# Fetching each expert row as two indirect DMAs, one per table, instead of one

## The reference

```
# scores of 8 heads against two sets of 128 keys; the best 16 of each; the best 16 of the 256 sums
idx = cand_i[best 16]                 # 16 expert numbers for each token and head, out of 16384
g   = softmax(top_s)
u   = take(u_tab, idx)                # 16384 x 1024 float32
a   = gelu(dot(u, h))                 # one number for each token and expert
vv  = take(v_tab, idx)                # 16384 x 1024 float32
out = sum over 128 experts of (g * a) * vv
```

## Time and profile before

| | |
|---|---|
| median of 3 runs | 2637.37 us (2637.25 to 2637.92) |
| the profiled execution, its own time | 2638.77 us |
| its span, first to last instruction | 2637.0 us |
| first expert row issued to last one landed, first layer | 1204.36 to 1854.20 us |
| the same in the second layer | 1962.49 to 2614.21 us |
| PE, DVE, ACT, POOL busy | 88%, 58%, 28%, 22% |

### The profile page before, as it was taken

One profiled execution on the slowest core, in us unless ns is written; L12 is line 12 of the kernel. 1 busy time (PEld: TensorE's weight loads), 2 busy tenths in 40 slices (PEclk: granted clock), 3 DMA queues, 4 the chain that ended last, 5 costly groups with the idle time before them and its releaser, 6 DMA issues.

```text
span 2637.0 us, 24279 instructions
## 1 busy us (share of the span) xinstructions
PE 2324.4 (88%) x8188; PEld 1496.0 (57%) x8188; DVE 1528.5 (58%) x3683; ACT 742.6 (28%) x2126; POOL 581.6 (22%) x526
## 2 busy tenths in 40 slices
PE   8999999999989999998998777877889988778776
PEld 6688888876878888566443323322674433233222
DVE  3743642255446413446777778776448777677774
ACT  2232100122120013333333333432324333233332
POOL 0000000000000000003453443543014443534431
PEclk9999999999999999999999999999999999999999
DMA  7315586442438754217999999999649999999996
GB/s 294 131 36 216 193 307 269 175 148 85 159 124 315 300 198 160 96 64 322 420 419 417 420 412 421 403 421 421 252 176 420 420 420 420 415 419 414 409 421 259
DMA packets 92317, 777.45 MB, mean 295 GB/s; under 512 B 10272, under 2 KB 11424, under 8 KB 11936
## 3 DMA queue, kind: packets, MB, share of 16 engines
q0 software_dynamic: 73728, 536.90, 49.3%
q1 hardware_dynamic: 18464, 238.99, 23.7%
HBM read 774.80 MB, written 1.05 MB: 294 GB/s over the span
## 4 chain that ended last, share of the span: by engine, by line
DMA 28%; PE 19%; POOL 5%; DVE 5%; issue 3%; ACT 2%; POOLq 0%; ACTq 0%
DMA weight_ring<-tables,arena 16%; DMA arena<-tables,arena 11%; PE misc L1371 7%; PE tile L295 3%; PE tile L1297 3%; POOL arena L1527 3%; POOL weight_ring L1527 2%; PE tile L308 2%; DVE weight_ring L1501 1%; DVE arena L1501 1%; PE tile L1648 1%; PE tile L1647 1%; PE misc L1671 1%; PE tile L318 1%; ACT arena L1453 0%
## 5 line engine op out<-in xcount | busy, mean ns | idle before, releaser
L1371 PE MATMUL misc<-arena 128*128 128x512 f32 x1216 | 586.1, 619 | 141.6 <-ACT arena L1453 141.5
L1527 POOL DMA_INDIRECT arena<-tables,arena x304 | 322.9, 1062 | 1031.4 <-DVE arena L1149 882.4
L1371 PE MATMUL misc<-weight_ring,arena 128*128 128x512 f32 x832 | 393.6, 611 | 106.5 <-ACT arena L1453 106.2
L1501 DVE CUSTOM_DVE_ANT_0 arena<-arena,memT 128x1024 f32<-128x1024 f32 x304 | 371.2, 1225 | 189.2 <-DMA arena<-tables,arena 186.1
L1371 PEld LDWEIGHTS misc<-arena 128*128 128x128 f32 x1216 | 226.3, 195 | 434.8 <-ACT arena L1453 227.2
L295 PE MATMUL tile<-xT,weight_ring 128*128 128x256 f32 x1792 | 388.6, 379 | 0.0
L295 PEld LDWEIGHTS tile<-xT,weight_ring 128*128 128x128 f32 x1792 | 340.3, 190 | 47.9 <-issue 1.8
L1527 POOL DMA_INDIRECT weight_ring<-tables,arena x208 | 255.8, 1230 | 429.4 <-DVE arena L1149 366.0
L1501 DVE CUSTOM_DVE_ANT_0 weight_ring<-weight_ring,memT 128x1024 f32<-128x1024 f32 x208 | 254.2, 1224 | 149.3 <-DMA weight_ring<-tables,arena 148.7
L1371 PEld LDWEIGHTS misc<-weight_ring,arena 128*128 128x128 f32 x832 | 150.6, 192 | 321.8 <-ACT arena L1453 181.1
L1439 ACT ACTIVATE arena<-arena 128x2 f32<-128x2 f32 x256 | 52.1, 204 | 813.0 <-DVE arena L1501 812.9
(11 more groups left out here) (261 smaller groups left out, 2279.7 us busy)
## 6 DMA issues: line engine op xcount, KB each, us to landing
weight_ring<-panels SPq DMA_DIRECT2D x110, 2048.0 KB, 7.8
arena<-tables,arena POOLq DMA_INDIRECT x304, 15.0
weight_ring<-tables,arena POOLq DMA_INDIRECT x208, 18.9
arena<-c_rows SPq DMA_DIRECT2D x2, 1024.0 KB, 21.3
cst<-consts SPq DMA_DIRECT2D x1, 1224.0 KB, 26.6
xT<-acts SPq DMA_DIRECT2D x1, 1024.0 KB, 5.0
memT<-acts SPq DMA_DIRECT2D x1, 1024.0 KB, 11.5
arena<-acts SPq DMA_DIRECT2D x1, 1024.0 KB, 13.3
```

The lines of the kernel that those rows point to most:

```text
L1371: ins = nc.tensor.matmul(M[2 * a + b][:, :], diag[:, s % NDIAG, :], slot(rows, s)[:, D + b * 512:D + (b + 1) * 512], start=first_row, stop ...
L1501: nc.vector.tensor_tensor_reduce(out=u, in0=u, in1=ht[:, n // PH, :], scale=1.0, scalar=0.0, op0=ALU.mult, op1=ALU.add, accum_out=dot[:, c ...
L1527: pool.indirect_dma_start(slot(rows, s), None, tables, bass.IndirectOffsetOnAxis(idx[:, n % 2, k:k + 1], 0)).then_inc(landing(rows, s), 16)
```

## The change

The joined table is taken apart into `table_u` and `table_v`. Each row is fetched by two indirect DMAs of 4 KB to a partition, u first and then v, with the same expert numbers and into the same places as before. Each slot has two semaphores now, one for u and one for v. DVE waits for u alone, and PE has a wait for v ahead of its matmuls. The order of the rows, the slots and all other work stay as they are. The further lines reuse 22 semaphores of the first block, which has ended by then, since each slot needs one more.

```diff
+        spare = []
+
         def sem(name):
             if name not in sems:
-                sems[name] = ctx.enter_context(nc.semaphore(name))
+                sems[name] = spare.pop() if spare else ctx.enter_context(nc.semaphore(name))
             return sems[name]
...
+        for name in ("low_filled", "low_read", "z_filled", "z_made", "act_gate", "bc_made", "bd_made", "ep_made", "en_made",
+                     "ed_made", "kd_made", "qe_made", "kdt_filled", "kdt_read", "att_filled", "att_masked", "tap_added",
+                     "conv_made", "state_half", "osq_made", "gated", "o_scaled"):
+            spare.append(sems.pop(name))
...
-        def landing(rows, s):
+        def landing(rows, s, part):
             kind, i = rows.place[s]
-            return sem(f"row_landed{i if kind == 'near' else HOME + i}")
+            return sem(f"row_landed_{part}{i if kind == 'near' else HOME + i}")
...
                 pe.wait_ge(sem("diag_made"), HEADS * TOPK * l + s + 1)
+                pe.wait_ge(landing(rows, s, "v"), 16 * rows.landed[s])
...
-                    dve.wait_ge(landing(rows, s), 16 * rows.landed[s])
+                    dve.wait_ge(landing(rows, s, "u"), 16 * rows.landed[s])
...
-                pool.indirect_dma_start(slot(rows, s), None, tables,
-                                        bass.IndirectOffsetOnAxis(idx[:, n % 2, k:k + 1], 0)
-                                        ).then_inc(landing(rows, s), 16)
+                at = bass.IndirectOffsetOnAxis(idx[:, n % 2, k:k + 1], 0)
+                pool.indirect_dma_start(slot(rows, s)[:, 0:D], None, table_u, at
+                                        ).then_inc(landing(rows, s, "u"), 16)
+                pool.indirect_dma_start(slot(rows, s)[:, D:2 * D], None, table_v, at
+                                        ).then_inc(landing(rows, s, "v"), 16)
...
-            "tables": np.concatenate([a["peer_u_2"], a["peer_v_2"]], axis=2).reshape(DEPTH * NEXP, 2 * D),
+            "table_u": a["peer_u_2"].reshape(DEPTH * NEXP, D), "table_v": a["peer_v_2"].reshape(DEPTH * NEXP, D),
```

More of the change, by code:

```diff
@@ L205, in at, with build_program @@
         return n % NBANK, n // NBANK
-def build_program(nc, panels, vec_a, vec_b, consts, mask_in, acts, tables, c_rows, out):
+def build_program(nc, panels, vec_a, vec_b, consts, mask_in, acts, table_u, table_v, c_rows, out):
     with ExitStack() as ctx:
```

## The result

The kernel after takes 2807.23 us (median of 4 executions, 2804.28 to 2814.37) against 2637.64 for the kernel before in the same measurement: 1.0635 times as long, with a 95% interval of 1.0621 to 1.0648. That is 170 us more. The forecast was 2812 and slower. The ratios, here and in the table of the experiments, leave out executions more than 1.5% above the fastest of their kernel, which matters for the halves by partition alone: their ratio is that of the two fastest of four executions, 3450.97 and 3490.50 us.

A forecast was written before the change was run, and what follows sets the result against it. The DMA engines were taken to bound the kernel before, POOL's issues the one after. +177.5 us for the slower rows less 2.9 for the early u made +174.6, on the median 2637.37 us 2812; range 2650 to 2920.

The forecast's parts named there:

- The bound: Expert steps: POOL needs 2.87 us a row against the DMA engines' 2.54 and becomes the bound; chance 0.66.
- The price of an issue: POOL's issue of half the bytes costs the full price, 1.130 us plus a 0.305 us gap, twice a row.
- The hold: POOL's issue starting inside a DVE dot product waits for its end: mean 1.13 us against median 0.94.
- The sum by layer: First issue to last landing of each layer grows to 739.5 us: 89.7 + 87.8 = 177.5 us extra.
- the terms of the forecast: End of a layer: issue 0.94 us, then 5.1 to landing, then 6.07 to the closing copy less about 1.4.
- The thin cover: Next head's expert numbers arrive about POOL's 15th row of 16; one row late would cost 86 us over 30 heads.
- The early u: End of each layer: DVE waits for u alone, which lands 1.43 us ahead of v; -2.9 us in all.
- The packets: DMA engines: 4 KB packets cost a row the same as 8 KB ones, at most 20 us more in 512 rows.
- the case in which the stream stays the bound: Expert steps: issue with gap below 1.27 us, so the DMA engines still set the pace; 2635 to 2655 us, chance 0.15.
- The share of DMA: Expert steps after the change: DMA engines' busy share falls to 2.54/2.87, 0.88, at 365 GB/s.

The follow-up runs named there:

- the halves by partition: Kernel before with each row fetched by two indirect DMAs of 64 partitions each, all 8 KB wide: 3502.92 us, 1.314 times the kernel before.
- the last pair: Kernel before with only the last two rows of each layer split, in the order u254, u255, v254, v255: 2637.5 us, ratio 0.9988.
- the one-input kernel: Kernel after with the dot product replaced by a plain sum of u, one SBUF input instead of two: 2670.18 us, ratio 1.0113.

## Why the prediction was right

**The bound.** That POOL becomes the bound was right, and is shown from both sides: fewer bytes change nothing, more issues cost in proportion, and issues that are not held give four fifths of the time back. All of the loss lies in the expert steps: the rest of the span is 1323.3 us before and 1323.0 after.

**The price of an issue.** Forecast 1.130 + 0.305 us, taken from the mean of before; measured 1.120 + 0.304. The u issues, of half the bytes, have the median of before, 0.937 us. For two issues that is 2.85 us a row instead of 2.87. That an issue of half the bytes costs the same was an argument in the prediction, since no row showed one; the runs bear it out.

**The hold.** That the mean hold carried over from before, 0.19 us beyond the median, to 0.18 is in part luck. The prediction backed it by scaling the 0.25 us of a head with the share of time that DVE is in a dot product, 42/49, and this scaling fails with four issues a row: there the share is 1.225/5.75, or 21%, which would give 0.11 us, and 1.133 - 0.947 = 0.19 was measured. The rule for a single issue holds with one exception. Of the issues of the kernel after, 308 begin 0.1 to 1.0 us after the start of such an instruction of 128 x 1024, and all are held. Of the 20 that begin in its first 0.1 us, the ten within 0.041 us of its start are not held, and the ten from 0.045 us on are; they take up to 1.99 us.

**The sum by layer.** From the first issue to the closing copy, before: 655.9 and 657.8 us (the second closing copy of before is at 2620.28). The prediction's terms give 739.5 + 4.6 = 744.1 for each. The closing copies after:

```profile
1939.37 0.69 DVE L1211 COPY memT<-misc 128x512 f32<-128x512 f32 x1 [4.83 <-PE misc L1379]
...
2784.98 0.69 DVE L1211 COPY memT<-misc 128x512 f32<-128x512 f32 x1 [4.83 <-PE misc L1379]
```

With first issues at 1202.81 and 2042.98 they make 736.6 and 742.0. The extra is 80.7 + 84.2 = 164.9 us where 174.6 was forecast, and the span grew by 164.6. The ten us are in what the issues are held: 2.84 and 2.86 us a row instead of 2.87. The median grew by 169.6, as the executions of after spread over 10 us; the profiled one was the fastest of them. The stretch from the last v issue to the closing copy is 10.7 us in the first layer (from 1928.66) and 11.4 in the second (from 2773.59), and the terms of the forecast, 0.94 + 5.11 + 4.64, make 10.7. In the first layer this hides that the last v issue was held, 1.48 us instead of 0.94, and that what follows took half a us less than forecast.

**The thin cover.** The next head's numbers never came late: no wait for L1156 inside a layer.

**The early u.** -2.9 us was not resolved in the times by undoing it. In one profiled execution of each, from the end of the last issue to the closing copy, it is 9.2 and 10.5 us in the two layers with the early u and 11.7 and 10.8 without, 2.8 us in sum but unevenly. Where POOL has time, the last pair, it is worth 3.2 us.

**The packets.** Here a term was mis-sized, hidden by POOL. From the output's store I read that 4 KB packets cost the DMA engines nothing, 20 us at most, and gave 2635 to 2655 for the case in which the stream stays the bound. Measured in that case: 34.4 us, 2670. The store's mean of 0.1406 us a packet came from a transfer that had the engines for itself and writes memory instead of reading it, and it was set against the mean of 8 KB packets in a full stream; in the full stream of the one-input kernel a packet of the expert rows has 50.7% of 16 x 2665.7 us / 147456 = 0.147 us. The Trainium skill, page DMA: Bandwidth & Descriptors, section iDMA fabric, has 408.7 GB/s for a load stream of 4 KiB rows, and the estimate from it, 2.57 us a row, was the nearer: the trace agrees, with 410 GB/s.

**The share of DMA.** Forecast 0.88 at 365 GB/s, measured 0.98 at 369 and 367. A packet has 51.1% of 16 x 2801.6 us / 147456 = 0.155 us here, more than the 0.147 us in the full stream, so part of the share is time in which a packet waits; for what, no run tells.

## What to carry to other kernels

Splitting a DMA that GpSimd issues costs one more issue, 1.24 us of POOL and more where a VectorE instruction with two SBUF inputs is under way; before splitting, hold the doubled price against the time that the stream needs for the same bytes. A half that lands earlier was worth something here only where the consumer waits for that piece and not for the pace of a full stream: split the last transfer, not each. A DMA share near 1 does not show that the DMA engines are the bound; look at GB/s, and at whether the issuing engine ever waits.

## What the runs showed of the hardware

- What an indirect DMA costs POOL hardly depends on what it moves: medians of 0.937 us for 8 KB and for 4 KB a partition, 0.946 to 0.948 for 2 KB and 0.944 for 512 bytes; 0.897 us for 64 partitions of 8 KB instead of 128.
- A one-input TENSOR_REDUCE of 1.22 us holds no issue; the two-input dot product of the same length holds one that begins inside it until 0.81 us after its end, unless less than 0.13 us of it is left. A two-input TENSOR_TENSOR of 0.42 us holds an issue too (1.14 us at 1327.04), a one-input MATCH_REPLACE8 of 0.41 us that writes as much does not (0.94 at 1322.01).
- Which of the two goes first is decided within hundredths of a microsecond: an issue that begins up to 0.041 us after the start of the dot product is not held, and the dot product takes 1.26 to 1.30 us instead of 1.22; one that begins 0.045 us after it is held and takes 1.99 us (kernel after, ten issues of each kind).
- A full stream of 4 KB packets moves 410 GB/s, one of 8 KB packets 421, both with one semaphore packet to eight of data; one of 8 KB packets to 64 partitions at a time 226 to 241 in three windows of 100 us.
- With packets of 512 bytes and 4 KB mixed, the DMA engines show a share of 0.68 while moving 200 GB/s, less than half the rate of the full stream.
